# Two-layer block plus a gated-linear and latent-attention block on one core: a reordered front, and the feed-forward's wide and narrow products grouped over a tile's two units

## What is computed

```python
def gated_deltanet(hn, ...):                       # hn = rmsnorm(x)
    proj = hn @ w_in                                # q, k, v, z, b, a
    qkv = jax.nn.silu(causal_dwconv(qkv, conv_w))   # width 4
    q, k = l2norm(q), l2norm(k)
    beta = sigmoid(b); g = -exp(a_log) * softplus(a + dt_bias)

def conv_gated_mlp(hn, w_up, conv_w, conv_b, w_down):   # twice, width 3
    u = causal_dwconv(hn @ w_up, conv_w, conv_b)
    gate, val = jnp.split(u, 2, axis=-1)
    return (jax.nn.silu(gate) * val) @ w_down

f = (silu(h @ w_ffn_gate) * (h @ w_ffn_up)) @ w_ffn_down  # once, no convolution
```

## Time and profile before

| | |
|---|---|
| median of three runs | 1174.02 us (1173.6 to 1174.33) |
| profiled execution, its own time | 1174.0 us |
| span of the profiled execution | 1171.9 us |
| PE matmul busy | 99% of the span |
| POOL, ACT, DVE busy | 74%, 63%, 52% |
| granted TensorE clock, mean | 0.998 |

### The profile page before, as it was taken

One profiled execution on the slowest core, in us unless ns is written; L12 is line 12 of the kernel. 1 busy time (PEld: TensorE's weight loads), 2 busy tenths in 40 slices (PEclk: granted clock), 3 DMA queues, 4 the chain that ended last, 5 costly groups with the idle time before them and its releaser, 6 DMA issues.

```text
span 1171.9 us, 21463 instructions
## 1 busy us (share of the span) xinstructions
PE 1158.4 (99%) x7040; PEld 1004.5 (86%) x7040; DVE 614.0 (52%) x1638; ACT 735.5 (63%) x1440; POOL 869.1 (74%) x374
## 2 busy tenths in 40 slices
PE   8999999999999999999999999999999999999997
PEld 7998899888888889878888888988798888888886
DVE  5667767536655566447655555291362426323234
ACT  6777677656766667757766667664375546655453
POOL 5846744377988887637988889878778465988883
PEclk9999999999999999999999999999999999999999
DMA  7678522256766566525665565666557343666550
GB/s 290 193 151 202 179 89 92 72 180 198 251 187 195 188 190 186 172 64 162 215 197 188 188 197 163 198 191 204 160 164 233 107 145 126 214 195 193 187 179 37
DMA packets 60776, 202.84 MB, mean 173 GB/s; under 512 B 6160, under 2 KB 12560, under 8 KB 60576
## 3 DMA queue, kind: packets, MB, share of 16 engines
q1 hardware_dynamic: 53424, 193.37, 51.8%
q10 hardware_dynamic: 7280, 8.52, 4.0%
HBM read 197.67 MB, written 4.19 MB: 172 GB/s over the span
## 4 chain that ended last, share of the span: by engine, by line
PE 96%; DVE 2%; ACT 1%; issue 1%; DMA 0%; DVEq 0%; ACTq 0%
PE bank L185 18%; PE bank L187 17%; PE bank L186 17%; PE solve L200 10%; PE bank L200 9%; PE solve L210 5%; PE bank L210 5%; PE bank L1007 1%; PE solve L1021 1%; PE bank L1593 1%; PE bank L194 1%; PE bank L1616 1%; PE solve L1602 0%; PE bank L1899 0%; PE bank L1900 0%
## 5 line engine op out<-in xcount | busy, mean ns | idle before, releaser
L169 POOL TENSOR_TENSOR wlo<-raw,whi 128x1024 fp32r<-128x1024 f32 x361 | 860.0, 2410 | 279.0 <-ACT whi L165 275.7
L165 ACT ACTIVATE whi<-raw 128x1024 fp32r<-128x1024 f32 x361 | 379.5, 1057 | 124.9 <-PE bank L187 122.7
L185 PE MATMUL bank<-whi,xpair 128*128 128x512 f32 (+2 forms) x456 | 178.4, 391 | 0.1
L187 PE MATMUL bank<-whi,xpair 128*128 128x512 f32 (+2 forms) x456 | 173.9, 381 | 0.0
L186 PE MATMUL bank<-wlo,xpair 128*128 128x512 f32 (+2 forms) x456 | 173.8, 381 | 0.0
L200 PE MATMUL solve<-xpair,whi 128*128 128x512 f32 x528 | 137.3, 392 | 0.2
L200 PE MATMUL bank<-xpair,whi 128*128 128x512 f32 x480 | 124.6, 391 | 0.0
L185 PE MATMUL bank<-xpair,whi 128*128 128x256 f32 (+1 forms) x408 | 120.7, 296 | 0.9 <-issue 0.5
L186 PE MATMUL bank<-xpair,whi 128*128 128x256 f32 (+1 forms) x408 | 116.0, 284 | 0.0
L187 PE MATMUL bank<-xpair,wlo 128*128 128x256 f32 (+1 forms) x408 | 116.0, 284 | 0.0
L200 PEld LDWEIGHTS solve<-xpair,whi 128*128 128x128 f32 x528 | 97.0, 189 | 18.3 <-issue 1.0
(11 more groups left out here) (460 smaller groups left out, 1870.3 us busy)
## 6 DMA issues: line engine op xcount, KB each, us to landing
raw<-in_stream SPq DMA_DIRECT2D x363, 512.0 KB, 3.5
band_scratch<-band ACTq DMA_DIRECT2D x1, 3072.0 KB, 36.3
area<-band_scratch ACTq DMA_DIRECT2D x2, 1024.0 KB, 8.2
resid<-in_x SPq DMA_DIRECT2D x2, 512.0 KB, 4.8
scr<-in_row_b_gate ACTq DMA_DIRECT2D x1, 1024.0 KB, 4.9
out<-resid SPq DMA_DIRECT2D x4, 256.0 KB, 2.0
tab<-in_tabs SPq DMA_DIRECT2D x1, 640.0 KB, 7.0
area<-in_row_final ACTq DMA_DIRECT2D x1, 512.0 KB, 4.5
```

The source lines that it names most:

```text
L165: act.activation(whi[:, n.s, :], raw[:, n.s, :], ACT.Copy).then_inc(hi_ready, 1)
L169: pool.tensor_tensor(wlo[:, n.s, :], raw[:, n.s, :], whi[:, n.s, :].bitcast(F32), ALU.subtract).then_inc(lo_ready, 1)
L185: nc.tensor.matmul(out_ap, a_hi, b_hi, start=start, stop=False)
L187: return nc.tensor.matmul(out_ap, a_lo, b_hi, start=False, stop=stop)
```

## The change

In the feed-forward, `up(j)` now issues the eight wide products of the gate unit, the eight wide ones of val, then the eight narrow ones of gate and the eight narrow ones of val. `bcast_root` is handed to the val unit's narrow products. In the front, the transposes of x are issued as five of the first half, then second and first half in turn; `turn_gates` moves behind tile 0, the spreading of the root into tile 1 behind seven of its eight k steps (one k step earlier than before); `turn_block(2)` moves from behind tile 4 to behind tile 5; ACT rounds unit 5 before it waits for the root, and unit 6 right after it copied the root (it was after the silu of tile 0), takes the Exp later, and makes the masks at tile 7 in place of tile 2.

```diff
-        def pairs_still(pe, n, bank, on_the_way=None, at=0):
-            def high(k):
-                return pe.matmul(bank[:, 0:2 * SEQ], whi[...], xpair[:, k, :], start=k == 0, stop=k == KD - 1)
+        def high_products(pe, n, bank):
             pe.wait_ge(hi_ready, n.u + 1)
-            for k in range(KD - 1):
-                high(k)
+            for k in range(KD):
+                pe.matmul(bank[:, 0:2 * SEQ], whi[...], xpair[:, k, :], start=k == 0, stop=False)
+        def low_products(pe, n, bank, on_the_way=None, at=0):
+            pe.wait_ge(lo_ready, n.u + 1)
             for k in range(KD):
                 if on_the_way and k == at:
                     on_the_way()
-                if k == 0:
-                    pe.wait_ge(lo_ready, n.u + 1)
-                pe.matmul(bank[:, 0:SEQ], wlo[...], xhi[:, k, :], start=False, stop=False)
-            high(KD - 1).then_inc(unit_done, 1)
+                mm = pe.matmul(bank[:, 0:SEQ], wlo[...], xhi[:, k, :], start=False, stop=k == KD - 1)
+            mm.then_inc(unit_done, 1)
...
-                    pairs_still(pe, ffn_unit(f, j, i, what), ffn_bank(j, half), None if half else on_the_way, 0 if conv else 5)
+                    high_products(pe, ffn_unit(f, j, i, what), ffn_bank(j, half))
+                for half, what in enumerate(("gate", "val")):
+                    low_products(pe, ffn_unit(f, j, i, what), ffn_bank(j, half), on_the_way if half else None, 0 if conv else 5)
...
-                    weights_still(pe, unit(BASE["qk"] + b), [...], KD, 0, turn_gates if b == 1 else None)
-                if b == 1:
-                    pe.wait_ge(CV.root, 1)
-                    (spread the root)
+                    weights_still(pe, unit(BASE["qk"] + b), [...], KD, 0, spread_root if b == 1 else None, 7)
+                if b == 0:
+                    pe.wait_ge(GT.copied, 1)
+                    (turn the gates)
...
-                if b == 4:
-                    turn_block(pe, 1)
-                if b >= 3:
-                    turn_block(pe, 0 if b == 3 else b - 2)
+                if 3 <= b < 6:
+                    turn_block(pe, b - 3)
+                if b >= 5:
+                    turn_block(pe, b - 2)
...
                 if b == 1:
-                    refill(act, BASE["ba"])
                     refill(act, BASE["qk"])
-                if b == 2:
+                if b == 7:
                     masks(act)
...
-            for k in range(KD):
-                pe.transpose(ps[k][:, 0:P], resid[:, 0, k * P:k * P + P], ident)
+            for k in range(5):
+                turn_first(0, k)
             pe.wait_ge(IN.x1, 16)
             for k in range(KD):
-                pe.transpose(ps[k][:, P:SEQ], resid[:, 1, k * P:k * P + P], ident).then_inc(TR.turned, 1)
+                turn_first(1, k).then_inc(TR.turned, 1)
+                if k + 5 < KD:
+                    turn_first(0, k + 5)
...
             round_unit(act, unit(3))
-            act.activation(small[:, 16:32], small[:, 16:32], ACT.Exp).then_inc(GT.rates, 1)
             gates_copy(act)
             round_unit(act, unit(4))
+            act.activation(small[:, 16:32], small[:, 16:32], ACT.Exp).then_inc(GT.rates, 1)
+            round_unit(act, unit(5))
             act.wait_ge(CV.bcast, 1)
             act.activation(rbc[:], ps[6][:, 0:SEQ], ACT.Copy).then_inc(CV.root_copied, 1)
-            round_unit(act, unit(5))
+            refill(act, BASE["ba"])
```

More of the change, by code:

```diff
@@ L195, in both @@
             return nc.tensor.matmul(bank[:, 0:SEQ], w_lo, xhi[:, k, :], start=False, stop=False)
-        def pairs_still(pe, n, bank, on_the_way=None, at=0):
-            def high(k):
-                return pe.matmul(bank[:, 0:2 * SEQ], whi[:, n.s, k * P:k * P + P], xpair[:, k, :], start=k == 0, stop=k == KD - 1)
+        def high_products(pe, n, bank):
             pe.wait_ge(hi_ready, n.u + 1)
-            for k in range(KD - 1):
-                high(k)
+            for k in range(KD):
+                pe.matmul(bank[:, 0:2 * SEQ], whi[:, n.s, k * P:k * P + P], xpair[:, k, :], start=k == 0, stop=False)
+        def low_products(pe, n, bank, on_the_way=None, at=0):
+            pe.wait_ge(lo_ready, n.u + 1)
             for k in range(KD):
@@ L207, in pairs_still, with weights_still @@
                     on_the_way()
-                if k == 0:
-                    pe.wait_ge(lo_ready, n.u + 1)
-                pe.matmul(bank[:, 0:SEQ], wlo[:, n.s, k * P:k * P + P], xhi[:, k, :], start=False, stop=False)
-            high(KD - 1).then_inc(unit_done, 1)
-        def weights_still(pe, n, outs, kts, xs, on_the_way=None):
+                mm = pe.matmul(bank[:, 0:SEQ], wlo[:, n.s, k * P:k * P + P], xhi[:, k, :], start=False, stop=k == KD - 1)
+            mm.then_inc(unit_done, 1)
+        def weights_still(pe, n, outs, kts, xs, on_the_way=None, at=2):
             pe.wait_ge(lo_ready, n.u + 1)
@@ L224, in weights_still @@
                     i += 1
-                    if on_the_way and i == 2:
+                    if on_the_way and i == at:
                         on_the_way()
@@ L824, in qk_pe, with spread_root @@
             mm.then_inc(unit_done, 1)
-            def turn_gates():
-                pe.wait_ge(GT.copied, 1)
+            def spread_root():
+                pe.wait_ge(CV.root, 1)
                 for t in range(NT):
-                    mm = pe.transpose(ps[7][:, t * 32:t * 32 + 32], cba[0:32, t * P:t * P + P], ident[0:32, 0:32])
-                mm.then_inc(GT.ba, 1)
+                    mm = pe.matmul(ps[6][:, t * P:t * P + P], root_of("a")[:, t:t + 1].broadcast_to([P, P]), ident,
+                                   start=True, stop=True)
+                mm.then_inc(CV.bcast, 1)
             for b in range(16):
@@ L847, in qk_pe @@
                 else:
-                    weights_still(pe, unit(BASE["qk"] + b), [proj_bank(b)[:, 0:SEQ]], KD, 0, turn_gates if b == 1 else None)
-                if b == 1:
-                    pe.wait_ge(CV.root, 1)
+                    weights_still(pe, unit(BASE["qk"] + b), [proj_bank(b)[:, 0:SEQ]], KD, 0, spread_root if b == 1 else None, 7)
+                if b == 0:
+                    pe.wait_ge(GT.copied, 1)
                     for t in range(NT):
-                        mm = pe.matmul(ps[6][:, t * P:t * P + P], root_of("a")[:, t:t + 1].broadcast_to([P, P]), ident,
-                                       start=True, stop=True)
-                    mm.then_inc(CV.bcast, 1)
+                        mm = pe.transpose(ps[7][:, t * 32:t * 32 + 32], cba[0:32, t * P:t * P + P], ident[0:32, 0:32])
+                    mm.then_inc(GT.ba, 1)
                 if b == 6:
@@ L2482, in start_pe, with turn_first @@
             pe.wait_ge(IN.x0, 16)
-            for k in range(KD):
-                pe.transpose(ps[k][:, 0:P], resid[:, 0, k * P:k * P + P], ident)
+            def turn_first(t, k):
+                return pe.transpose(ps[k][:, t * P:t * P + P], resid[:, t, k * P:k * P + P], ident)
+            for k in range(5):
+                turn_first(0, k)
             pe.wait_ge(IN.x1, 16)
             for k in range(KD):
-                pe.transpose(ps[k][:, P:SEQ], resid[:, 1, k * P:k * P + P], ident).then_inc(TR.turned, 1)
+                turn_first(1, k).then_inc(TR.turned, 1)
+                if k + 5 < KD:
+                    turn_first(0, k + 5)
         def start_act(act):
```

## The result

The changed kernel takes 1182.92 us (median of four runs, 1181.08 to 1183.08) against 1173.81 us for the kernel before (four runs, 1173.15 to 1174.33): the ratio is 1.0076, 95% interval 1.0063 to 1.0088. It is slower by 9.1 us; 1182.7 was forecast. The profiled execution took 1182.82 us, with a span of 1180.7; its span is 8.8 us longer than that of before.

What follows compares the result with a forecast made beforehand. PE was taken as the bound everywhere, with a product running 99% of the span. Front -1.6, grouping -1.1, heads +9.3 and clock +2.1 gave +8.7 on 1174.0: 1182.7 us, range 1177.5 to 1187.5.

Steps and rivals of the forecast that it cites:

- Regrouping: Feed-forward products: fewer steps from narrow to wide over 21 tiles in each of three feed-forwards, -1.1 us, bounds 0 and -1.6.
- the 0.017 us: Saving per tile in the feed-forwards from one fewer narrow-to-wide step, taken 63 times.
- the tail's cover: Feed-forward tail: tile 19's chain ends later, cover before up(21) shrinks from 2.0 to 0.2 us; cost taken as 0.
- The late broadcast: Heads of the three feed-forwards: root's broadcast 3.0 us later, so PE waits in up(2), +9.3 us in all.
- 2.6 + 0.9: Convolution feed-forward heads, up(2): PE waits 2.6 us for gate's last tap, then 0.9 us more for val's.
- 0.4 at up(3): Convolution feed-forward heads: a wait of 0.3 to 0.4 us before up(3) that the later PE no longer has.
- 2.9 in the last: Last feed-forward's head: up(2) waits 2.0 us for gate's silu and 0.8 to 0.9 for val, 2.9 in all.
- The front: Before the feed-forwards: old wait gone, new one at turn_block(3), -1.6 us; -0.9 if the clock falls, -2.4 if it holds.
- The new wait for the copy of the keys: Front, turn_block(3): PE waits about 2.1 us for the first keys' copy, 1.6 us sooner than before; starts at 32.0.
- The half of the clock's price: Front: low clock after the 2.1 us wait would lose 1.5 us; half was taken, giving -1.6 us.
- The clock: Three heads: low clock after up(2)'s waits, 0.7 us each on average, +2.1 us, bounds 0 and 4.8.
- The Trainium skill's way to price a low stretch: Throttled time times one minus the clock's ratio: 1.7 us for 3.4 us in the kernel before, against about 1.5 traced.

Runs made afterwards that it cites:

- the clean pair of kernels: `both_early` repeated, 1167.67 us, beside the same kernel with products in the order of before, 1168.76 us.
- late_root_alone: Kernel before, with only the root's broadcast of up(1) handed to val's narrow products, product order unchanged: 1182.22 us, before 1173.94.
- group_only: Kernel before with the change's grouped products, broadcast left behind gate's wide products, front as before: 1173.22 us, before 1173.94.
- root_back: Changed kernel with the broadcast back behind seven wide gate products (nine in the last feed-forward): 1171.34 us, before 1173.94.
- low_part_first: Changed kernel, but ACT takes tile 0's low parts, and DVE adds them, before ACT copies the root: 1175.93 us, before 1174.0.
- front_only: Changed kernel with the feed-forwards of before, so only the front is changed: 1171.82 us, before 1173.94.
- wait_filled_short: Changed kernel with three unused fp32 products of 512 columns (two in the last feed-forward) before up(2)'s wait: 1181.32 us, before 1173.4.
- turns_late: `root_back` with turn_block kept three tiles behind the projections up to tile 10, where two are made at once: 1168.98 us, before 1174.0.
- both_early: `turns_late` plus tile 0's low parts ahead of the root's copy, as in `low_part_first`: 1167.63 us, before 1174.0.
- the two in the old order: `both_early` and `turns_late`, each with feed-forward products in the order of before: 1168.76 and 1169.41 us.
- wait_filled: Changed kernel with five unused fp32 products of 512 columns (four in the last feed-forward) before up(2)'s wait: 1181.69 us, before 1174.0.

## Why the prediction was right, point by point

- **Regrouping: -1.1 forecast.** The three stretches behind the heads are 0.45, 0.49 and 0.38 us shorter, 1.3 in all, and the clean pair of kernels gives 1.1. So the size is shown. That it is the step from narrow to wide products that costs the 0.017 us is argued from a few rows of one tile, which are themselves rounded to 0.01; no run varied the number of steps by another amount. The loop of the feed-forward got no wait, as argued from its slack of 11 us, and the tails none either: gate's later `unit_done` is covered in the loop. The forecast called the tail's cover 0.2 us; tile 19's product ended at 436.91 + 0.43 = 437.34 and up(21) started at 437.49, so it was 0.15.
- **The late broadcast: +9.3 forecast, without the clock.** With the clock held up by filler the heads are 18.02, 18.02 and 17.35 us against 14.63, 14.63 and 14.41: 3.4 + 3.4 + 2.9 = 9.7 us. The terms were 2.6 + 0.9 (measured 2.43 and 0.72 between products, with the restart on top) less 0.4 at up(3), and 2.9 in the last. `late_root_alone` shows that the place of the broadcast is enough for a loss of 7.4 of these 9.7 us, `group_only` and `root_back` that without it there is no loss, and `low_part_first` that the chain behind the root carries it. The other 2.3 us need the grouping too. The forecast counted them right, since it took val's wait from the new order of products, but it did not say that grouping made the late broadcast dearer.
- **The front: -1.6 forecast, between -0.9 and -2.4.** The new wait for the copy of the keys is 2.03 us where 2.1 was worked out, and it ends at 31.9 where 32.0 was; the copy itself came 1.8 us sooner (31.45 against 33.26), forecast 1.6. In the profiled run the clock fell behind the wait and up(1) came 1.0 us sooner; in `root_back`, where it held, 2.4. These are the two bounds, -0.9 and -2.4. `front_only` as a median gained 2.1. The half of the clock's price that I took was the mean of two cases that both occur, and no run sits on it.
- **The clock: +2.1 forecast in the heads.** It fell behind both waits of 2.43 us and not behind the last head's 1.8; the price was 0.60 and 0.78 us, 1.4 in all. That term was 0.7 too dear, because I spread it over three heads.
- **Terms that made up for one another.** In the profiled run -1.0 - 1.3 + 9.7 + 1.4 = +8.8. Forecast: -1.6 - 1.1 + 9.3 + 2.1 = +8.7. The errors are +0.6 in the front, -0.2 in the grouping, +0.4 in the heads and -0.7 in the clock. That the total came out 0.1 us off is luck. It also rests on the low clock in the front of the profiled execution, which three of the four times seem to share; without it an estimate is 1182.8 - 1.4 = 1181.4 us, and the fourth time is 1181.08. That each term lies within 0.7 us is not luck.
- The Trainium skill's way to price a low stretch, which the prediction set beside its own (page "TensorE: Matmul & The Clock Gate", section Terms), gives as an estimate 1.7 us for 3.4 us at half clock. Where PE had only work in the stretch, the runs give 1.3 to 1.6 (two groups of times in four kernels); where a wait stood in it, 0.6 to 0.8. In these runs it was an upper bound.

What stays open: why the clock falls in some executions and not in others behind the same wait of 2.0 us, and in `late_root_alone` behind one wait of 2.20 us and not behind the other. The records show that it happens, not why.

## What to carry to other kernels

An instruction that is slipped into the middle of another's work, here a broadcast handed through as an argument, must be followed by its own consumers when the work around it is reordered. Ask when the result is ready, who idles for it now (the row of ACT said 3.54 us), and what stands in front of it in the new order. And when a wait is removed, work out the next one: the front's 2.5 us wait gave way to one of 2.0 us one tile later, and only moving the turn behind the copy it needs brought the whole gain. A gain of 1.1 us was real and a loss of some 10 us came with it in the same edit, and the loss was larger than either edit would have made it alone. So they are best timed apart and together.

## What the runs showed of the hardware that I had not expected

- The same wait of PE brings the low clock in one execution and not in the next. `root_back` has eight times at 1171.2 to 1171.5 and two at 1172.8 to 1172.9; `front_only`, `low_part_first` and `wait_filled_short` show such groups as well, 1.3 to 1.6 us apart. The kernels without a wait over 1 us in this place (`turns_late`, `both_early` and the two in the old order) scatter by only 0.3 us; but so do the four times of `wait_filled`, which has the wait of 2.0 us and a mean clock of 0.999 to 1.0 in all four. In `group_only` even the old wait, 2.49 us, left the clock up in the profiled run. Its timeline row, and then the window behind it:

```profile
29.26 0.44 PE L818 MATMUL solve<-tab,area 128*128 128x128 f32 x2 [2.49 <-ACT area L909]
```

```profile
30.00:33.40 3.40, 2.77 (x25) 2.60 (x23) 2.77 (x7) 3.14 (x12) 3.40 (x3) 1.00 0.79 243
```

- A plain fp32 product of 512 columns holds PE 0.78 us (3.89 us for five in `wait_filled`), where one on rounded operands takes 0.23 (seven in 1.58 us); as filler it is 3.4 times as long as a wide product of this kernel.
